# A ring of weight chunks loaded as three pairs of 2 MB in place of six single chunks of 1 MB

## The reference, cut to what matters

```
x = first_block(x, ...)        # 2 layers: SwiGLU FFN (1024 -> 2 x 2816 -> 1024), three attention mixers with
                               # gates, SwiGLU FFN; final rmsnorm
for i in range(2):             # second_block, streams x and ctx (256 rows each)
    shift, scale, gate = adaln_params(c, ada_w[i], ada_b[i])
    x = x + gate * (fourier_mix(hx) if i == 0 else rwkv(hx, ctx))
    x = x + gate * ec_moe(hx, router[i], wg[i], wu[i], wd[i])     # and ctx the same way when i == 0

def ec_moe(h, router, wg, wu, wd):          # 16 experts, each takes 32 rows of a stream
    gates, idx = lax.top_k(swapaxes(softmax(h @ router)), 32)
    xs = h[idx]                                             # [16, 32, 1024]
    hid = silu(xs @ wg) * (xs @ wu)                         # wg, wu: 1024 x 1024 for each expert
    ys = (hid @ wd) * gates                                 # wd: 1024 x 1024
    return zeros.at[idx].add(ys)
```

## Time and profile before

| | |
|---|---|
| median of 3 runs | 3063.11 us (3060.39 to 3065.65) |
| the profiled execution | 3063.15 us |
| its span in the trace | 3060.9 us |
| TensorE busy | 2769.2 us, 90% of the span |
| DMA, mean over the span | 231 GB/s, 707.09 MB |
| ring loads | 625 of 1 MB |

### The profile page before, as it was taken

How to read it: one execution, slowest core, us unless ns; L and a number is a source line. 1 busy time by engine, 2 the same in 40 slices (tenths; PEclk the granted TensorE clock), 3 DMA queues, 4 the chain that set the end, 5 groups by cost and what they waited for, 6 DMA issues and landing times.

```text
span 3060.9 us, 57418 instructions
## 1 busy us (share of the span) xinstructions
PE 2769.2 (90%) x25016; PEld 1834.5 (60%) x25016; DVE 1164.2 (38%) x1613; ACT 975.7 (32%) x1496; POOL 177.7 (6%) x231
## 2 busy tenths in 40 slices
PE   8999999999998999999999988999999997866765
PEld 6877877878777878865333333446777774433322
DVE  4545565545455565432010012434555534000001
ACT  4435555444345555422101001113444431100000
POOL 0003000000002000000000000002222220000000
PEclk9999999999999999999999999999999998888777
DMA  6474344565652355525999999711000027999997
GB/s 262 171 278 155 105 150 179 198 262 181 254 209 102 120 209 185 188 91 215 405 422 421 421 421 413 286 67 63 10 16 10 10 75 303 375 421 420 421 421 325
DMA packets 101398, 707.09 MB, mean 231 GB/s; under 512 B 11780, under 2 KB 12548, under 8 KB 18224
## 3 DMA queue, kind: packets, MB, share of 16 engines
q1 hardware_dynamic: 91008, 658.22, 54.8%
q10 hardware_dynamic: 9504, 42.86, 3.6%
q0 software_dynamic: 656, 2.52, 0.2%
HBM read 702.47 MB, written 1.07 MB: 230 GB/s over the span
## 4 chain that ended last, share of the span: by engine, by line
PE 67%; DMA 18%; DVE 7%; ACT 6%; issue 2%; SPq 0%; POOL 0%; ACTq 0%; DVEq 0%; POOLq 0%
DMA weight_ring<-in_stream 18%; PE banks L2030 9%; PE banks L650 7%; PE banks L652 7%; PE banks L651 7%; PE banks L1869 3%; PE banks L2394 3%; PE banks L1016 3%; PE banks L1018 2%; PE banks L1017 2%; PE banks L2440 2%; ACT front L1280 1%; PE banks L1176 1%; PE banks L2805 1%; PE banks L2816 1%
## 5 line engine op out<-in xcount | busy, mean ns | idle before, releaser
L2030 PE MATMUL banks<-weight_ring,scratch 128*32 128x256 f32 (+1 forms) x4312 | 574.3, 513 | 149.8 <-DMA weight_ring<-in_stream 132.4
L2030 PEld LDWEIGHTS banks<-weight_ring,scratch 128*32 128x32 f32 (+1 forms) x4312 | 186.1, 130 | 502.6 <-DMA weight_ring<-in_stream 236.6
L647 DVE TENSOR_TENSOR split_high<-weight_ring,split_high 128x1024 fp32r<-128x1024 f32 x198 | 242.7, 1230 | 262.6 <-ACT split_high L642 262.2
L642 ACT CAST split_high<-weight_ring 128x1024 fp32r<-128x1024 f32 x198 | 207.3, 1052 | 294.6 <-PE banks L652 235.8
L2181 DVE TENSOR_TENSOR scratch<-scratch,banks 128x512 f32<-128x512 f32 (+1 forms) x32 | 17.7, 554 | 560.0 <-PE banks L2030 560.0
L1368 DVE TENSOR_TENSOR split_high<-weight_ring,split_high 128x1024 fp32r<-128x1024 f32 x128 | 161.5, 1272 | 161.5 <-ACT split_high L1265 161.5
L3176 ACT COPY scratch<-banks 128x1024 f32<-128x1024 f32 (+2 forms) x192 | 143.7, 782 | 212.3 <-PE banks L2808 156.9
L650 PE MATMUL banks<-split_high,features_low 128*128 128x512 f32 x480 | 189.8, 395 | 0.0
L652 PE MATMUL banks<-split_high,features_high 128*128 128x512 f32 x480 | 187.1, 390 | 0.0
L651 PE MATMUL banks<-split_high,features_high 128*128 128x512 f32 x480 | 186.8, 389 | 0.0
L1265 ACT CAST split_high<-weight_ring 128x1024 fp32r<-128x1024 f32 x128 | 133.4, 1049 | 166.3 <-PE banks L1018 160.3
(11 more groups left out here) (422 smaller groups left out, 4639.3 us busy)
## 6 DMA issues: line engine op xcount, KB each, us to landing
weight_ring<-in_stream SPq DMA_DIRECT2D x625, 1024.0 KB, 10.4
scratch<-in_kept ACTq DMA_DIRECT2D x19, 1024.0 KB, 9.8
scratch<-in_pair_rows ACTq DMA_DIRECT2D x8, 448.0 KB, 3.6
scratch<-in_kept ACTq DMA_DIRECT2D x6, 512.0 KB, 5.5
scratch<-in_lora ACTq DMA_DIRECT2D x2, 1536.0 KB, 17.6
front<-in_gain_rows ACTq DMA_DIRECT2D x5, 512.0 KB, 3.8
bias<-bias_rows POOLq DMA_DIRECT2D x1, 2304.0 KB, 14.1
scratch<-in_routing ACTq DMA_DIRECT2D x1, 1040.5 KB, 5.1
```

Of the source, the lines that this page charges most:

```text
L642: act.copy(split[i % 4][0], source(i)).then_inc(*self.rounded.up())
L647: dve.tensor_tensor(lo, source(i), hi.bitcast(F32), ALU.subtract).then_inc(*self.rest.up())
L2030: last = pe.matmul(self.psum[q * M:(q + 1) * M, (GATE, UP, DOWN)[part], 0:W], left, w[j][:, q * W:(q + 1) * W], start=(k == 0), stop=(k == ...
```

## The change

The ring keeps its six chunks, 6 MB. It is now loaded as three pairs. One DMA of 2 MB brings chunks 2p and 2p + 1 into neighbouring slots. The host lays each pair out so that a partition's 16 KB are contiguous in HBM (before: 8 KB). One semaphore stands for a pair, so that the reader of either chunk waits for both. The load of pair p waits until both chunks of the pair before it in the same place are used. As 625 is odd, the last load brings one chunk; a chunk of zeros pads the stream in HBM.

```diff
-        self.slot_loaded = [... nc.semaphore(f"slot_loaded{i}")) for i in range(RING)]
+        self.pair_loaded = [... nc.semaphore(f"pair_loaded{i}")) for i in range(PAIRS)]
...
     def wait_chunk(self, pe, chunk):
-        pe.wait_ge(self.slot_loaded[chunk % RING], 16 * (chunk // RING + 1))
+        pe.wait_ge(self.pair_loaded[chunk // 2 % PAIRS], 16 * (chunk // RING + 1))
...
+            def pair_slot(s):
+                return self.ring[:, s * 2 * CHUNK:(s + 1) * 2 * CHUNK]
+
+            for s in range(PAIRS):
+                sp.dma_start(pair_slot(s), stream[s]).then_inc(self.pair_loaded[s], 16)
             with sp.Fori(1, self.chunk // RING) as turn:
-                for s in range(RING):
-
-                    sp.wait_ge(self.chunks_used.sem, turn * RING + (s + 1 - RING))
-                    sp.dma_start(self.slot(s), stream[turn * RING + s]).then_inc(self.slot_loaded[s], 16)
+                for s in range(PAIRS):
+                    sp.wait_ge(self.chunks_used.sem, turn * RING + (2 * s + 2 - RING))
+                    sp.dma_start(pair_slot(s), stream[turn * PAIRS + s]).then_inc(self.pair_loaded[s], 16)
...
+            for p in range(self.chunk // RING * PAIRS, (self.chunk + 1) // 2):
+                s, n = p % PAIRS, min(2, self.chunk - 2 * p)
+                sp.wait_ge(self.chunks_used.sem, 2 * p + 2 - RING)
+                sp.dma_start(pair_slot(s)[:, 0:n * CHUNK], stream[p, :, 0:n * CHUNK]).then_inc(self.pair_loaded[s], 16)
...
+    ring = np.delete(stream, kept, 0)
+    ring = np.concatenate([ring, np.zeros((len(ring) % 2, P, CHUNK), f)])
+    a = {"stream": ring.reshape(-1, 2, P, CHUNK).transpose(0, 2, 1, 3).reshape(-1, P, 2 * CHUNK), ...
```

More of the change, by code:

```diff
@@ L35 @@
 RING = 6
+PAIRS = RING // 2
 HD = 64
@@ L213, in __init__ @@
         self.psum = ctx.enter_context(nc.psum_tensor("banks", [P, 8, NB], F32))
-        self.slot_loaded = [ctx.enter_context(nc.semaphore(f"slot_loaded{i}")) for i in range(RING)]
+        self.pair_loaded = [ctx.enter_context(nc.semaphore(f"pair_loaded{i}")) for i in range(PAIRS)]
         self.chunks_used = signal("chunks_used")
@@ L328, in _ @@
         def _(sp):
-            for s in range(RING):
-                sp.dma_start(self.slot(s), stream[s]).then_inc(self.slot_loaded[s], 16)
+            def pair_slot(s):
+                return self.ring[:, s * 2 * CHUNK:(s + 1) * 2 * CHUNK]
+            for s in range(PAIRS):
+                sp.dma_start(pair_slot(s), stream[s]).then_inc(self.pair_loaded[s], 16)
             with sp.Fori(1, self.chunk // RING) as turn:
-                for s in range(RING):
-                    sp.wait_ge(self.chunks_used.sem, turn * RING + (s + 1 - RING))
-                    sp.dma_start(self.slot(s), stream[turn * RING + s]).then_inc(self.slot_loaded[s], 16)
-            for c in range(self.chunk // RING * RING, self.chunk):
-                sp.wait_ge(self.chunks_used.sem, c + 1 - RING)
-                sp.dma_start(self.slot(c), stream[c]).then_inc(self.slot_loaded[c % RING], 16)
+                for s in range(PAIRS):
[5 more added lines that the diff above has]
+                sp.dma_start(pair_slot(s)[:, 0:n * CHUNK], stream[p, :, 0:n * CHUNK]).then_inc(self.pair_loaded[s], 16)
     def norm_rows(self, tiles, xn, src=None):
@@ L3622, in layout @@
     kept = [start + at for start, places in zip((first, second), KEPT_AT) for at in places]
-    a = {"stream": np.delete(stream, kept, 0), "kept": stream[kept], "x": i["x"][0], "ctx": i["ctx_2"][0], "ident": np.eye(P, dtype=f)}
+    ring = np.delete(stream, kept, 0)
+    ring = np.concatenate([ring, np.zeros((len(ring) % 2, P, CHUNK), f)])
+    a = {"stream": ring.reshape(-1, 2, P, CHUNK).transpose(0, 2, 1, 3).reshape(-1, P, 2 * CHUNK), "kept": stream[kept], "x": i["x"][0], "ctx": i["ctx_2"][0], "ident": np.eye(P, dtype=f)}
     a["gain_rows"] = np.stack([i[n][l] for l in range(DEPTH) for n in ("norm_ffn1", "norm_mix", "norm_ffn2")])
```

## The result

The changed kernel takes 3106.42 us (median of 4 runs, 3104.39 to 3114.08) against 3064.19 us before: a ratio of 1.0144, 95% interval 1.0132 to 1.0157. It is 42 us slower where I had forecast 8. Its first profiled execution took 3114.08 us, well above its other three. So I profiled the same kernel a second time; that execution took 3108.07 us, the kernel's median there was 3106.02 us (4 runs), 43.4 us above the 3062.67 of before. Its windows differ from the first profile's in one place: in 2680 to 3000 us the first had 414 GB/s, the second 422.

The account below looks back on a forecast made before the run. The two expert stages were taken as bound by weight loads at full DMA rate. Waits of 17.8 us less 9 us of faster transfer gave +8.8, kept as +8: 3071 us from 3063, range 3056 to 3086 us.

Parts of the forecast that it names:

- The start: Kernel start: ACT's first cast waits for the whole pair, at about 14.2 us instead of 11.76; +2.4 us, never regained.
- The rate: DMA-bound stretches, 927 us: fewer, longer packets make transfers 1% faster; -9 us, with ends of -18 and +5.
- Between the stages: Conditioning weights, where PE outruns the loads twice: pairs land later, +2.5 and +3.5 us; together +6.0 us (3 to 7).
- The second stage: Second expert stage: +2.4 us at entry, with five chunks there instead of six, and +1 us for the ring running dry.
- The ring can run dry: Mainly first expert stage: PE must free a pair within 7.7 us instead of 10.2; some experts exceed it; 3 us (0 to 9).
- the entry and PE's lag: First expert stage: +1.7 us for the first ring load's later issue, +1.3 us for pairs done later; together +3.0 (0 to 4).
- the lone load: Load on an idle queue: 4.8 us for one chunk, 2.3 of it not transfer; a lone pair should land after 7.3 us.
- A: Rival, whole kernel: waits mostly covered and transfers gain 18 us, so faster, about 3050 us; chance 0.12.
- B: Rival, whole kernel: no gain from longer rows and all losses, 18 to 22 us, giving 3083 us; chance 0.17.
- C: Rival, 170 pairs: 16 KB packets are slow, 1.0 us each, 8 us a pair instead of 4.98; about 3580 us; chance 0.02.
- D: Rival, first expert stage: regrouped waits lower PE's clock for a fifth of the time; +38 us, 3110 us; chance 0.04.
- The signs: Named signs: windows at 425 GB/s, first cast at 14.2 us, second expert stage about 14 us later, DMA share dipping under 1.0.

Follow-up runs that it names:

- lightest pair kernel: The changed kernel with ten of every sixteen products of the experts' matmuls left out; 3072.02 us.
- two-load kernel: Changed kernel's order, pair issued and waited for as one, but as two 1 MB loads with 8 KB per partition; 3111.01 us, ratio 1.0159 to the kernel before.

## Why the prediction was wrong

*Where the bound lies: right.* The expert stages set it, and before 1430 us nothing changed but the start.

*The start, +2.4: right.* The first cast now begins at 14.34 us (14.2 forecast), and 2.4 us are still there at 1432 us.

*The rate, 1%: nearly right.* It is 1.4% in the second stage of the lightest pair kernel, where the ring is nearly always full; in the changed kernel's own second stage it is 422 against 421 GB/s. With the ring partly dry in the first stage it could not be earned there.

*Between the stages, +6.0: right in size*, 7.1 measured.

*The second stage, +3.4 less 4 for the rate: right in its waits, without the gain.* The entry waits for a load of 7.77 us in place of 5.38, 2.4 us more, as worked out; in all the stage adds 2.8 us.

*"The ring can run dry", 3 us with an end of 9: this step failed.* Together with the +3.0 of the entry and PE's lag it should have added 6, and it added 33 and ate the rate's gain. Its mechanism was named correctly. The size was wrong: I had a few experts go over by some tenths to 2 us, and held that PE's lag is otherwise worked off within an expert. The landing times show nearly every expert losing, 2.2 us on average. The cover is the term that was mis-sized. I took 9.96 - 2.3 = 7.7 us as if the DMA were one server, its 16 engines in step. The issue and landing times of six kernels put it at 5.5 to 6.2 us. With it, a need of 7.9 us goes over by about 2 us in nearly every expert, and 16 x 2 = 32 us is of the size measured. That the missing 1.5 to 2.2 us are the spread of the engines' finishes (S) is argued from their like size, 2.2 us; no run changes the spread alone. I should have doubted a difference of two large numbers that is nearly zero, because such a term belongs into the range at its full slope, not with an end of 9.

*A second, smaller fault* lies in the lone load: it takes 7.7 us (median of those in 300 to 600 us), 0.4 more than 4.8 + 2.49. The loss in the window has a like part: DMA share falls by 4% (1.01 to 0.97) but traffic by 6.7% (421 to 393), so about 10 of the 27 us lost there are not idle engines but longer packets. The packet records show them: 6% of the 16 KB packets in the window take over 1.2 times the median, and the mean is 646 ns for a median of 611; before, 0.1% do. In the two-load kernel with 8 KB packets it is 4%, at the same share and traffic (0.97, 392), so this does not need 16 KB rows. In the lone loads of 300 to 600 us the first 16 packets take 0.8 us on average with 8 KB and 1.3 us with 16 KB, where the medians are 0.31 and 0.61, and the later ones are near the medians; so the cost sits in the restart. Why the first packets are slow stays open. Part of what I give to S may be this.

The Trainium skill's rule of the largest transfer (SBUF — State Buffer, The DMA setup-cost knee), weighed ahead of the result, gave no gain here: the pair loads cost 42 us, and 5 of the two-load kernel's 48 us are all that the larger transfer brought.

*The rivals.* A is out. B had the losses at 18 to 22 us at most and the rate's gain at nothing: right in direction, half the size. C is out: 611 ns, not 1.0 us. D named 3110 us, which is within 4 us of the result, but by luck: its cause did not happen, the granted clock in the first stage is 0.98 to 1.00. The range, up to 3086, missed since it knew only ring terms of a few microseconds.

*The signs.* The first cast and the DMA share under 1.0 came as named. The rate did not: 402 and 410 GB/s in the two windows where 425 was named. The second expert stage began 42 us later and not 14.

No version here that does the whole work beats the kernel before: in its expert stages the engines never pause (421 GB/s, share 1.01), and the 1.4% that longer rows offer need the cover that the pairs take.

## What to carry to other kernels

A ring that feeds a stretch at full DMA rate is worth its cover. As an estimate, that is the transfer time standing behind the chunk in use, less the lead of a lone load, less the spread between the DMA engines' finishes (here 12.5 - 2.3 - 2.2 us; with three pairs 10.0 - 2.3 - 2.2; the runs put the last term at 1.5 to 2.2). Compare that with the longest run of work that the reader does without freeing anything. Below it every period loses about the difference: 2 us here, in nearly every expert. Read the need from the trace, as the time from a load's landing to the next issue for its place, and not from the jobs' shortest times. By those the lightest pair kernel needed 4.5 us, but it held 15 of 79 pairs for over 5.5 us. Coarser loads take from both sides at once, later use and later issue, and their gain in rate (1.4% here) is small once several loads stand in the queue.

## What the hardware showed that I had not expected

- The 16 engines' completions of one load lie 2.1 to 3.7 us apart (medians of the two windows in both kernels), about a whole load of 1 MB, where those of a lone 1 MB load lie 0.4 us apart. They go through the queue each at its own pace.
- A ring can lose 7% of its rate although it is empty for only 0.3 us in 400; the DMA share then reads 0.97 instead of 1.01.
- In the lone loads of 300 to 600 us the first 16 packets take 0.8 us on average with 8 KB and 1.3 us with 16 KB; the medians are 309 and 611 ns.
- Two costs of grain that make 12.7 and 18.7 us alone make 48.0 us together.
